# Expert gates of a two-layer transformer kernel: one-hot rows for eight tokens in 16-bit pairs, all on VectorE, tokens innermost in the apply

## The reference, cut to what matters

```
idx = take_along_axis(top_i[0] * 128 + top_i[1], best_pos)      # 128 picks per token
g   = softmax(best_s)
act = gelu(einsum('nd,nhkd->nhk', x, u_tab[idx]))
out = einsum('nhk,nhkd->nd', g * act, v_tab[idx])
```

## Time and profile before

| | |
|---|---|
| median of 3 runs | 3381.05 us (3377.15 to 3381.17) |
| profiled execution | 3373.28 us, its span 3371.3 us |
| PE busy | 3067.7 us (91%) |
| DVE busy | 2358.2 us (70%) |
| ACT busy | 1828.7 us (54%) |
| POOL busy | 1147.1 us (34%) |
| part 0, first layer | 424.9 to 669.5 us |
| part 1, first layer | 671.7 to 931.4 us |
| part 0, second layer | 1519.8 to 1765.1 us |
| part 1, second layer | 1767.2 to 2029.1 us |

### The profile page before, as it was taken

The page is one execution under the profiler, slowest core; times in us unless marked ns, Lnnn a source line. Parts: engine busy times, 40 slices in busy tenths (PEclk is TensorE's granted clock), DMA queues, the critical chain, the costliest instruction groups (busy, mean ns, idle before and its releaser), DMA issues.

```text
span 3371.3 us, 58728 instructions
## 1 busy us (share of the span) xinstructions
PE 3067.7 (91%) x21820; PEld 2730.0 (81%) x21820; DVE 2358.2 (70%) x4217; ACT 1828.7 (54%) x4063; POOL 1147.1 (34%) x883
## 2 busy tenths in 40 slices
PE   8899988888899889998888889979997999998899
PEld 7699988866688779998886668869876998977798
DVE  4559999899945555999989994564566545456644
ACT  5455566666555445556666555545544555554454
POOL 1113366666522111335666652222110223211121
PEclk9999999999999999999999999989999999999999
DMA  5345543433455325554343335545522555542254
GB/s 208 107 169 169 176 138 132 145 126 125 132 197 196 129 88 169 170 175 138 132 145 126 126 125 202 196 166 191 167 98 82 185 188 193 184 161 82 100 188 157
DMA packets 139532, 512.77 MB, mean 152 GB/s; under 512 B 15713, under 2 KB 16242, under 8 KB 137970
## 3 DMA queue, kind: packets, MB, share of 16 engines
q1 hardware_dynamic: 134352, 489.22, 43.4%
q10 hardware_dynamic: 4898, 19.81, 1.6%
HBM read 507.92 MB, written 1.05 MB: 151 GB/s over the span
## 4 chain that ended last, share of the span: by engine, by line
PE 59%; DVE 25%; issue 8%; POOL 3%; ACT 3%; DMA 1%; DVEq 0%; ACTq 0%; POOLq 0%; SPq 0%
PE ps L404 58%; DVE GAIN L2081 5%; DVE WL L1587 4%; DVE GAIN L2087 4%; DVE OHW L2094 2%; POOL WL L2321 2%; DVE GL L2112 2%; POOL OHW L2450 1%; ACT WH L1031 1%; PE ps L408 1%; ACT BIG L1127 1%; DVE BIG L1699 0%; DVE BIG L1748 0%; DMA RAW<-in_w 0%; DVE XTl L1626 0%
## 5 line engine op out<-in xcount | busy, mean ns | idle before, releaser
L1031 ACT ACTIVATE WH<-RAW 128x512 fp32r<-128x512 f32 x1866 | 1165.4, 628 | 1037.4 <-PE ps L404 1010.8
L2321 POOL TENSOR_TENSOR WL<-RAW,WH 128x512 fp32r<-128x512 f32 x585 | 870.5, 1488 | 2096.6 <-ACT WH L1031 2096.6
L1587 DVE TENSOR_TENSOR WL<-RAW,WH 128x512 fp32r<-128x512 f32 x1281 | 992.5, 779 | 777.7 <-ACT WH L1031 770.7
L404 PE MATMUL ps<-XTh,WH 128*128 128x256 f32 x3928 | 1139.4, 290 | 22.1 <-DVE XTl L1795 8.3
L404 PE MATMUL ps<-XTl,WH 128*128 128x256 f32 x3928 | 1123.1, 286 | 0.0
L404 PE MATMUL ps<-XTh,WL 128*128 128x256 f32 x3928 | 1122.1, 286 | 0.0
L404 PEld LDWEIGHTS ps<-XTh,WH 128*128 128x128 f32 x3928 | 765.5, 195 | 33.4 <-DVE WL L1587 14.1
L404 PEld LDWEIGHTS ps<-XTl,WH 128*128 128x128 f32 x3928 | 766.2, 195 | 3.1
L404 PEld LDWEIGHTS ps<-XTh,WL 128*128 128x128 f32 x3928 | 765.3, 195 | 0.0
L404 PE MATMUL ps<-WH,GH 128*128 128x512 f32 x1408 | 569.9, 405 | 70.4 <-DVE GL L2112 59.6
L404 PE MATMUL ps<-WL,GH 128*128 128x512 f32 x1408 | 553.4, 393 | 0.0
(11 more groups left out here) (181 smaller groups left out, 2679.9 us busy)
## 6 DMA issues: line engine op xcount, KB each, us to landing
RAW<-in_w SPq DMA_DIRECT2D x933, 512.0 KB, 3.3
BIG<-in_ln ACTq DMA_DIRECT2D x4, 1024.0 KB, 5.1
GAIN<-in_norms ACTq DMA_DIRECT2D x6, 512.0 KB, 4.2
BIG<-in_sk ACTq DMA_DIRECT2D x2, 1024.0 KB, 4.8
BIG<-in_na_bias ACTq DMA_DIRECT2D x2, 1024.0 KB, 10.5
BIG<-in_qk_gain ACTq DMA_DIRECT2D x2, 960.0 KB, 7.2
BIG<-in_memT ACTq DMA_DIRECT2D x4, 256.0 KB, 7.6
BIG<-in_xT ACTq DMA_DIRECT2D x1, 1024.0 KB, 5.1
```

The costliest lines, as they stand in the source:

```text
L404: return self.e.matmul(out, lhsT, rhs, start=start, stop=stop, skip_group_check=loose)
L1031: e.activation(wh, raw, ACT.Copy).then_inc(*c.hi.mark(j))
L1587: e.tensor_tensor(wl, raw, wh.bitcast(F32), ALU.subtract).then_inc(*c.lo_v.mark(j))
L2321: e.tensor_tensor(wl, raw, wh.bitcast(F32), ALU.subtract).then_inc(*c.lo_p.mark(j))
```

## The change

The gates are built for eight tokens at a time, in 32 steps (`NG`) of two half-steps, with 68 ticks in place of 66 (`2 * NG + 4`). `IOTA2` is a bfloat16 table in which each number stands twice. `OHA` and `OHB` now hold tokens in pairs innermost: `[4 pairs, n, 2 tokens]`, and the other operand (`AB` or `GT`) is read as a pair of tokens again and again. All three `OHW` are made by VectorE; `gates` of ScalarE and GpSimd only yield. TensorE reads `OHA` and `OHW` with a step of 2 elements; it does the same number of matmuls, 24 in a block every second tick. The apply loops over groups outside and tokens inside, so that `G` is read and written in runs of 8, and the bank with a step of 64. `low_on_pool` returns False in all of parts 0 and 1, where it gave every second half to GpSimd. `OHB` and one set of `OHW` move to space that lies under `GH`/`GL` (part 0) and under `XTl` (part 1).

```diff
         if up <= j < up + 4 * (128 - GP):
-            return j % 2 == 1
+            return False
...
-        self.OHA = oh[:, 0:1536].rearrange("p (r k n) -> p r k n", r=3, k=4)
-        self.OHB = oh[:, 1536:1536 + 8 * GP].rearrange("p (r k n) -> p r k n", r=2, k=4)
-        self.OHW = sb("OHW", [P, 2, 3, 4 * GP], BF)
+        self.OHA = oh.rearrange("p (r a n k) -> p r a n k", r=2, a=4, k=2)
+        self.OHW0 = sb("OHW", [P, 3, 8 * GP], BF)
+        self.IOTA2 = sb("IOTA2", [P, 128, 2], BF)
...
 TensorE
-                for k in range(4):
-                    o = (m0 % 8 + k) * GP
+                e.wait_ge(*c.weighted.at(stage, part, s))
+                ps = self.bank(4 + s % 2)
+                for k in range(8):
                     for i in range(3):
-                        m = self.mm(ps[:, o:o + GP], c.OHA[:, s % 3, k, :], c.OHW[:, r, i, k * GP:k * GP + GP], i == 0, i == 2)
+                        m = self.mm(ps[:, k * GP:k * GP + GP], c.OHA[:, s % 2, k // 2, :, k % 2], c.OHW[part][s % 2][i][:, k // 2, :, k % 2],
+                                    i == 0, i == 2)
...
 ScalarE: the loop over 66 steps with 4 activations each is gone
 GpSimd: the loop over 66 steps with one tensor_tensor each is gone
...
 VectorE
-            e.tensor_copy(c.GT0[:, tb], c.GT[:, 0, tb]).then_inc(*c.vec.mark())
...
+        ia = c.IOTA2[:, :, :].unsqueeze(1).to_broadcast([P, 4, 128, 2])
+        ib = c.IOTA2[:, part * GP:part * GP + GP, :].unsqueeze(1).to_broadcast([P, 4, GP, 2])
+        pairs = lambda x, n: x.rearrange("p (a k) -> p a k", k=2).unsqueeze(2).to_broadcast([P, 4, n, 2])
+        for step in range(2 * NG + 4):
+            s = step // 2
+            n8 = slice(8 * s, 8 * s + 8)
+            if step % 2 == 0 and s < NG:
+                if s:
+                    e.wait_ge(*c.weighted.at(stage, part, s - 1))
+                e.tensor_tensor(ohb, ib, pairs(c.AB[:, 1, n8], GP), ALU.is_equal).then_inc(*c.vec.mark(stage, "ohb", part, s))
+                if s >= 2:
+                    e.wait_ge(*c.gate.at(stage, part, s - 2))
+                e.tensor_tensor(c.OHA[:, s % 2], ia, pairs(c.AB[:, 0, n8], 128), ALU.is_equal).then_inc(*c.vec.mark())
+            elif step % 2 and s < NG:
+                e.wait_ge(*c.vec.at(stage, "ohb", part, s))
+                for i in range(3):
+                    event = c.weighted.mark(stage, part, s) if i == 2 else c.vec.mark()
+                    e.tensor_tensor(c.OHW[part][s % 2][i], ohb, pairs(c.GT[:, i, n8], GP), ALU.mult).then_inc(*event)
+            t = (step - 5) // 2
+            if step % 2 and t >= 0:
+                g = G[:, part * GP:part * GP + GP, 8 * t:8 * t + 8]
+                e.wait_ge(*c.gate.at(stage, part, t))
+                e.tensor_tensor(g, g, c.B[4 + t % 2][:, :].rearrange("p (n i) -> p i n", n=8), ALU.mult).then_inc(*c.gated.mark(stage, part, t))
```

More of the change, by code:

```diff
@@ L145, in __init__ @@
         self.XTh = sb("XTh", [P, 8, 256], FR)
+        with nc.sbuf_tensor("ROWS", [P, 4, 512], BF) as self.ROWS1:
+            pass
         self.XTl = sb("XTl", [P, 8, 256], FR)
@@ L151, in __init__ @@
         oh = self.GAIN[:, :].bitcast(BF)
-        self.OHA = oh[:, 0:1536].rearrange("p (r k n) -> p r k n", r=3, k=4)
-        self.OHB = oh[:, 1536:1536 + 8 * GP].rearrange("p (r k n) -> p r k n", r=2, k=4)
-        self.OHW = sb("OHW", [P, 2, 3, 4 * GP], BF)
+        self.OHA = oh.rearrange("p (r a n k) -> p r a n k", r=2, a=4, k=2)
+        self.OHW0 = sb("OHW", [P, 3, 8 * GP], BF)
         self.AB = sb("AB", [P, 2, 256], BF)
         self.GT = sb("GT", [P, 3, 256], BF)
-        self.GT0 = sb("GT0", [P, 256], F32)
+        self.IOTA2 = sb("IOTA2", [P, 128, 2], BF)
+        with nc.sbuf_tensor("ROWS0", [P, 4, 512], BF) as self.ROWS0:
+            pass
         self.GH = sb("GH", [P, 2, 256], FR)
@@ L161, in __init__ @@
         self.VM = sb("VM", [P, 2, 256], F32)
+        g8 = lambda x: x.rearrange("p (a n k) -> p a n k", a=4, k=2)
+        first = [g8(self.OHW0[:, i, :]) for i in range(3)]
+        self.OHW = [[first, [g8(x[:, i, :]) for i in range(3)]] for x in (self.ROWS0, self.ROWS1)]
+        self.OHB = [g8(x[:, 3, :]) for x in (self.ROWS0, self.ROWS1)]
         self.CST = sb("CST", [P, 256 + 8], F32)
@@ L183, in __init__ @@
         self.summed = signal("summed")
-        self.one, self.ohw_a, self.ohw_p, self.ohw_v = signal("one"), signal("ohw_a"), signal("ohw_p"), signal("ohw_v")
+        self.weighted = signal("weighted")
         self.gate, self.gated = signal("gate"), signal("gated")
@@ L384 @@
 RA, RB = 2.0, 2.2
+NG = 32
 ORDER = {"gla": [6, 7, 0, 1, 2, 3, 4, 5], "sb": [6, 7, 0, 1, 2, 3, 4, 5], "mix": list(range(8))}
@@ L826, in gates @@
         c, e = self.c, self.e
[L827 to L835, removed]
-                for k in range(4):
-                    o = (m0 % 8 + k) * GP
+        for step in range(2 * NG + 4):
+            s = (step - 3) // 2
+            if step % 2 and 0 <= s < NG:
+                e.wait_ge(*c.weighted.at(stage, part, s))
+                ps = self.bank(4 + s % 2)
+                for k in range(8):
                     for i in range(3):
-                        m = self.mm(ps[:, o:o + GP], c.OHA[:, s % 3, k, :], c.OHW[:, r, i, k * GP:k * GP + GP], i == 0, i == 2)
+                        m = self.mm(ps[:, k * GP:k * GP + GP], c.OHA[:, s % 2, k // 2, :, k % 2], c.OHW[part][s % 2][i][:, k // 2, :, k % 2],
+                                    i == 0, i == 2)
                 m.then_inc(*c.gate.mark(stage, part, s))
-                if s % 2:
-                    self.empty[b] = c.gated.at(stage, part, s)
+                self.empty[4 + s % 2] = c.gated.at(stage, part, s)
             yield 1
@@ L1358, in gates @@
     def gates(self, stage, part):
[L1359 to L1372, removed]
+        for _ in range(2 * NG + 4):
             yield 1
@@ L1377, in split_g @@
         c, e = self.c, self.e
-        e.wait_ge(*c.gated.at(stage, g // GP, 63))
+        e.wait_ge(*c.gated.at(stage, g // GP, NG - 1))
         if last is not None:
@@ L1433, in peer_stage @@
         if layer == DEPTH - 1:
-            e.wait_ge(*c.gate.at(stage, 1, 63))
+            e.wait_ge(*c.gate.at(stage, 1, NG - 1))
             self.fetch_gain(0)
@@ L1801, in start @@
         e.wait_ge(*c.load("cst"))
+        e.tensor_copy(c.IOTA2[:, :, :], c.IOTA.unsqueeze(2).to_broadcast([P, 128, 2])).then_inc(*c.vec.mark())
         self.pace.flush()
@@ L2069, in gates @@
         c, e, G = self.c, self.e, self.c.peer.G
-        ia = c.IOTA.unsqueeze(1).to_broadcast([P, 4, 128])
-        ib = c.IOTA[:, part * GP:part * GP + GP].unsqueeze(1).to_broadcast([P, 4, GP])
+        ia = c.IOTA2[:, :, :].unsqueeze(1).to_broadcast([P, 4, 128, 2])
+        ib = c.IOTA2[:, part * GP:part * GP + GP, :].unsqueeze(1).to_broadcast([P, 4, GP, 2])
+        pairs = lambda x, n: x.rearrange("p (a k) -> p a k", k=2).unsqueeze(2).to_broadcast([P, 4, n, 2])
+        ohb = c.OHB[part]
         if part == 0:
@@ L2073, in gates @@
             e.wait_ge(*c.vec.at(stage, "gt", 1))
[L2074 to L2091, removed]
+        else:
+            e.wait_ge(*c.used.at(BASE[stage] + 32 + 255))
@@ L2092, in gates @@
+        for step in range(2 * NG + 4):
+            s = step // 2
[4 more added lines that the diff above has]
+                e.tensor_tensor(ohb, ib, pairs(c.AB[:, 1, n8], GP), ALU.is_equal).then_inc(*c.vec.mark(stage, "ohb", part, s))
                 if s >= 2:
                     e.wait_ge(*c.gate.at(stage, part, s - 2))
-                e.tensor_tensor(c.OHW[:, s % 2, 2, :].rearrange("p (k n) -> p k n", k=4), c.OHB[:, s % 2],
-                                c.GT[:, 2, 4 * s:4 * s + 4].unsqueeze(2).to_broadcast([P, 4, GP]),
-                                ALU.mult).then_inc(*c.ohw_v.mark(stage, part, s))
@@ L2103, in gates @@
+            t = (step - 5) // 2
+            if step % 2 and t >= 0:
+                g = G[:, part * GP:part * GP + GP, 8 * t:8 * t + 8]
+                e.wait_ge(*c.gate.at(stage, part, t))
+                if t == 0:
                     e.wait_ge(*c.act.at(stage, "gelu", part * GP + GP - 1))
-                e.tensor_tensor(g, g, c.B[4 + (s // 2) % 2][:, :].rearrange("p (n i) -> p n i", n=8),
-                                ALU.mult).then_inc(*c.gated.mark(stage, part, s))
+                e.tensor_tensor(g, g, c.B[4 + t % 2][:, :].rearrange("p (n i) -> p i n", n=8), ALU.mult).then_inc(*c.gated.mark(stage, part, t))
```

## The result

The changed kernel takes 3195.3 us (median of 4 runs, 3194.0 to 3196.7) against 3379.1 us (3377.0 to 3381.2) for the kernel before: a ratio of 0.9456, 95% interval 0.944 to 0.9473, or 184 us less.

The account below looks back on a forecast made before the run. VectorE, stretched by GpSimd, bounds the four gate parts; afterwards TensorE, at 208 and 203 us a part. Per layer 411, both 822 against 1011.5: 189.5 us less, so 3192 from 3381, range 3165 to 3290.

Parts of the forecast that it names:

- What bounds: In the four gate parts: VectorE, with GpSimd in it, bounds before; TensorE bounds part 0 after, part 1 nearly level.
- The sum: Over the four gate parts: 822 us after against 1011.5 before, 189.5 us less.
- The gate blocks: TensorE's gate matmuls in each part: 0.33 us per block of twelve, 64 blocks, 21.1 us.
- the 1.3% for the clock: Part 0: TensorE's 205.4 us raised to 208 for a granted clock of 0.98 to 0.99.
- the 5.5 us of stops: Part 1: added to TensorE's 197.5 us because GL ties two nearly level engines, giving 203.
- The stretching: VectorE in part 0: 70 of 230.5 us busy is stretching by GpSimd, gone once GpSimd has no work.
- The rows: VectorE's gate rows for eight tokens: paired 16-bit operands run at double rate, 1.93 us a group (upper bound 3.61).
- rival A: No doubling on VectorE's rows, 3.61 us a group: 3310 us (3265 to 3345), chance 0.11.
- The apply: VectorE's apply, 512 f32 elements: 0.95 us start to start, between 0.60 and 1.27.
- Rival B: The hopping bank makes VectorE's apply cost near 2 us: 3247 us (3230 to 3290), chance 0.10.
- TensorE's step of 2: TensorE's gate matmuls read weights and columns 4 bytes apart: taken to cost nothing, with weight loads as the risk.
- Rival C: Stepped weights lose TensorE's fast load, 97 ns more per gate matmul: slower, 3477 us, chance 0.07.

Follow-up runs that it names:

- run 2: Changed kernel with rows laid out token by token, without pairs, still eight tokens an instruction on VectorE, TensorE's operands contiguous: 3269.8 us, 0.9695.
- run 5: Changed kernel with neither the pairs nor the new order of the apply: 3347.8 us, 0.9896.
- run 4: Changed kernel without the matmuls of each gate's third term, whose OHW is still made: 3159.2 us, 0.9358.
- run 7: Kernel before with GpSimd idle in parts 0 and 1, VectorE making all splits there and the second term: 3313.6 us, 0.98.
- run 6: Kernel before with all splits of parts 0 and 1 on VectorE, GpSimd keeping its gate rows: 3246.5 us, 0.9598.
- run 10: Kernel before with GpSimd's gate row (second term) made by VectorE, GpSimd keeping its splits: 3341.4 us, 0.9909.
- run 3: Changed kernel with the apply in its old order, tokens outside and groups 1 KB apart inside: 3200.0 us, 0.9471.
- run 11: Changed kernel again, nothing changed, measured on the same chip as run 9: 3192.6 us, 0.9454.
- run 8: Changed kernel with ScalarE's and VectorE's rows of groups 0, 1 and 64 made earlier: 3183.8 us, 0.9418.
- run 9: Changed kernel with rows of groups 0, 1 and 64 made earlier, 0 and 1 also ahead of group 127's half splits: 3178.2 us, 0.9417.

## Why the prediction was right

*What bounds.* VectorE with GpSimd in it before, TensorE after: shown by runs 2 and 5 (VectorE's cost returns in full once it passes TensorE's need) and 4 (36 us for 1024 matmuls).

*The sizes.* Part 0 was put at 208 us and took 209.4 and 209.6; part 1 at 203 and took 203.4 and 203.2. The sum gave 189.5 us, the parts lost 185.9, the medians 183.8. Both parts came out so well partly by luck. The gate blocks were priced too low. The prediction ended the block of twelve at the next weight load (604.88), but the next matmul starts later:

```profile
604.91 0.36 PE L404 MATMUL ps<-XTh,WH 128*128 128x256 f32 x1
```

So the block held TensorE for 0.36 us, not 0.33, and the one behind this f32 matmul started at 605.11, 0.20 us later and not 0.12. In the changed kernel a block holds TensorE for 0.74 us, not 0.66, and the first f32 matmul behind it for 0.31 in part 1 where the others take 0.23 (the rows of run 2), or 0.20 for 0.12 in part 0. Together that is some 5 us in each part that the sum lacks. In part 0 the 1.3% for the clock, 2.7 us, covered half of it: the clock there was 1.00. In part 1 the 5.5 us of stops did, and those don't exist: the waits show TensorE stopped for `GL` at the handovers only. The slow clock behind the handover, 1.6 us, is no further term, since the stretch that gave 1.378 us a half began with it too:

```profile
934.00:937.00 3.00, 3.00 (x9) 2.35 (x8) 0.00 (x0) 0.63 (x1) 0.85 (x1) 0.50 0.82 311
```

That leaves under 1 us of part 1 without a place.

*The stretching.* That its 70 us a part go with GpSimd's work was right as a sum and is shown by run 7. Charging it to GpSimd as a whole was too coarse: runs 6 and 10 show that it hangs on the splits, and that rows and splits together stretch VectorE more than the splits alone. My expectations for both runs failed on this, by 84 us and by 83 us. Run 6 shows where the short rows go when they are alone, beside the apply. A row takes 0.6 us of the apply's 1.3; a split takes 1.3 us and, unless it starts with the apply, reaches past it (argued, not tested). Why VectorE's next two-input instruction goes ahead of a waiting GpSimd row in run 6, and often behind it in the kernel before, stays open: no view shows who holds what.

*The rows.* The lower bound, 1.93 us a group, held: 683 and 418 ns for the single instructions, 0.60 and 0.33 start to start; rival A is out, and run 2 shows its case (3270, inside its range of 3265 to 3345). The Trainium skill's section 5.1 of "Vector Engine (DVE) Microarchitecture Reference" held in both halves: 417 ns for 512 elements with pairs, 686 with step 0, both 16-bit throughout.

*The apply.* The 0.95 was mis-sized: it costs 0.60 start to start, the lower bound. A bank read with a hop of 256 bytes runs at the full rate (678 ns, against 685 for a bank read in order); what cost time was the hop of 1 KB in `G` (1332 ns in run 3, where the bank is read in order). The estimate from section 5.2 of the same page of the Trainium skill was near 1.0 us; 678 ns differs, and the measurement decides (the page measured SBUF). Rival B is out. It had no effect on the time, since TensorE bounds (run 3), so an error here was free.

*TensorE's step of 2.* 0.025 us in a block of 24 (run 2), 0.8 us in a part, where nothing was taken; weight loads have median 97 ns against a mean of 98. Rival C is out, and "TensorE: Matmul & The Clock Gate", section Weight-path perf modes, of the Trainium skill agrees.

## What to carry to other kernels

When an engine is busy without a break, ask what its instructions cost undisturbed before you look for work to take off it: here nearly a third of VectorE's busy time in these parts (70 of 230 us) was GpSimd's doing, and handing VectorE 38 us more work in each part, one changed line, made the kernel 4% faster. Then count savings only down to the next engine's need: the new apply saved 78 us with VectorE as the limit and 5 us without, and what remained worth having was elsewhere, in four stops of about 2 us each, with a fall of the clock behind them: 14 us together.

## What the runs showed of the hardware

- A two-input VectorE instruction on 16-bit operands takes two elements in the time of one with an innermost run of two elements re-read (`[4, 64 x step 0, 2]`): 512 elements in 417 ns, where 256 took 412 in the kernel before, and 686 ns for 512 with one element re-read (run 2). With 1024 elements it took 683 ns; the form of run 2, whose table of numbers is in f32, took 1219.
- GpSimd and VectorE slow each other unevenly. With only 256-element rows on GpSimd (run 6), VectorE's means stayed at 415 and 685 ns and GpSimd's rose to 1661 ns, where its shortest takes 607; most rows got through beside the apply, VectorE's one instruction there with a single SBUF input. With only 512-element splits on GpSimd (run 10), both lost: VectorE's 685 became 811 ns, and GpSimd's split took 2426 ns, where it takes 1297 undisturbed. With both kinds VectorE's 256-element instruction rose from 415 to 793 ns.
- Stops of TensorE of 1.84 and 2.23 us at the handovers were mostly, but not always, followed by 3.4 us with the granted clock at 0.50, the lower level of 1.2 GHz, which began within 1.3 us after work resumed. In the changed kernel it came behind all four. In run 3 it did not come behind the two stops of 1.84 us, in run 4 not behind the two of 2.23, and in run 11, the changed kernel again, not behind one of 2.23. It did not come behind the two stops of 1.74 us in run 8. With no stop (run 9) the clock stayed at 1.00 through the same change of work.
